# A gather asked for ahead of the accumulating scatter, and a one-hot sum as one matmul, in a mixture-of-experts trunk kernel

## The reference, cut to what matters

```
logits = (tok @ w_router + b_router)
top_logit, top_e = lax.top_k(logits, 4)
gate_w = softmax(top_logit)
# per expert, for the tokens that chose it:
gu = xs @ w_gu[e] + b_gu[e];  g, u = gu[:, :1024], gu[:, 1024:]
g = min(g, 7);  u = clip(u, -7, 7)
act = (u + 1) * (g * sigmoid(1.702 * g))
out = (act @ w_down[e] + b_down[e]) * gate_w
y = segment_sum(out, token)          # four rows are added up for each token
```

## Time and profile before

| | us |
|---|---|
| median of 3 runs | 2640.77 |
| lowest and highest | 2635.83, 2645.7 |
| the profiled execution, its own time | 2641.59 |
| its span, first to last instruction | 2639.9 |
| TensorE busy in the span | 2405.0 (91%) |
| VectorE, ScalarE, GpSimd busy | 1545.6, 1337.7, 835.9 |
| mean granted TensorE clock | 0.965 of full speed |

### The profile page before, as it was taken

One profiled execution on the slowest core, in us unless ns is written; L12 is line 12 of the kernel. 1 busy time (PEld: TensorE's weight loads), 2 busy tenths in 40 slices (PEclk: granted clock), 3 DMA queues, 4 the chain that ended last, 5 costly groups with the idle time before them and its releaser, 6 DMA issues.

```text
span 2639.9 us, 55169 instructions
## 1 busy us (share of the span) xinstructions
PE 2405.0 (91%) x19141; PEld 1347.5 (51%) x19142; DVE 1545.6 (59%) x1828; ACT 1337.7 (51%) x1395; POOL 835.9 (32%) x945
## 2 busy tenths in 40 slices
PE   6999988899989949899899998889988999999991
PEld 3555544667755535455455554445544555545550
DVE  2222246566635665961953768999679715165975
ACT  1111144356532244862843658888678624165861
POOL 1212222410003354343332443434334423233422
PEclk9999989899999969999999999999999999999996
DMA  8000043430032285982964779999989925177974
GB/s 331 11 18 18 9 153 123 125 90 0 0 114 89 96 290 167 388 300 69 361 230 136 263 262 334 397 397 393 332 306 398 331 57 194 28 256 274 356 281 182
DMA packets 180248, 538.48 MB, mean 204 GB/s; under 512 B 20672, under 2 KB 37490, under 8 KB 180142
## 3 DMA queue, kind: packets, MB, share of 16 engines
q1 hardware_dynamic: 150620, 487.79, 48.7%
q0 software_dynamic: 26656, 46.85, 7.9%
q10 hardware_dynamic: 2916, 3.14, 0.4%
HBM read 493.11 MB, written 45.20 MB: 204 GB/s over the span
## 4 chain that ended last, share of the span: by engine, by line
PE 46%; DVE 6%; issue 6%; ACT 2%; DMA 2%; POOL 1%; ACTq 0%; DVEq 0%; POOLq 0%; SPq 0%
PE psum L2054 42%; DVE arena L1825 5%; PE psum L2043 2%; PE psum L2038 2%; PE psum L2032 1%; ACT arena L1647 1%; DMA arena<-in_w_down 1%; DVE arena L1919 0%; DVE arena L1884 0%; DVE arena L1920 0%; DMA expert_lists<-arena 0%; POOL expert_lists L1502 0%; DVE arena L1933 0%; ACT arena L1695 0%; DVE arena L1874 0%
## 5 line engine op out<-in xcount | busy, mean ns | idle before, releaser
L2054 PE MATMUL psum<-arena 128*64 128x512 bf16 x12528 | 1419.0, 382 | 72.2 <-DVE arena L1874 39.4
L2054 PEld LDWEIGHTS psum<-arena 128*64 128x64 bf16 x12528 | 714.3, 111 | 727.1 <-DVE arena L1825 53.7
L1825 DVE TENSOR_TENSOR arena<-arena 128x2048 bf16<-128x2048 f32 x384 | 862.8, 2287 | 184.5 <-ACT arena L1647 184.2
L1647 ACT ACTIVATE arena<-arena 128x2048 bf16<-128x2048 f32 x384 | 723.0, 1904 | 99.0 <-DVE arena L1825 70.0
L1557 POOL DMA_INDIRECT expert_sums<-arena x90 | 186.9, 2076 | 670.7 <-issue 648.2
L551 PE MATMUL psum<-arena 128*128 128x512 f32 (+2 forms) x864 | 298.9, 504 | 1.1 <-ACT arena L407 1.1
L551 PEld LDWEIGHTS psum<-arena 128*128 128x128 f32 x864 | 150.8, 190 | 133.8 <-issue 129.1
L1874 DVE TENSOR_TENSOR arena<-psum,arena 128x512 bf16<-128x512 f32 x87 | 59.9, 688 | 233.6 <-ACT arena L1689 233.6
L1528 POOL DMA_INDIRECT arena<-expert_inputs,arena x88 | 107.5, 1222 | 202.5 <-PE psum L2032 176.9
L1685 ACT ACTIVATE arena<-psum 128x1024 bf16<-128x1024 bf16 x87 | 88.6, 1018 | 154.8 <-issue 152.8
L1700 ACT ACTIVATE arena<-psum,arena 128x512 f32<-128x512 f32 x87 | 59.3, 682 | 202.1 <-PE psum L2054 202.1
(11 more groups left out here) (269 smaller groups left out, 2186.8 us busy)
## 6 DMA issues: line engine op xcount, KB each, us to landing
arena<-in_w_gu SPq DMA_DIRECT2D x256, 1024.0 KB, 16.0
arena<-in_w_down SPq DMA_DIRECT2D x128, 1024.0 KB, 13.8
arena<-in_w_ada SPq DMA_DIRECT2D x12, 2048.0 KB, 9.6
arena<-in_x_sample SPq DMA_DIRECT2D x16, 512.0 KB, 3.4
arena<-in_w_in SPq DMA_DIRECT2D x3, 2048.0 KB, 20.3
expert_sums<-arena SPq DMA_DIRECT2D x10, 512.0 KB, 6.4
expert_inputs<-arena SPq DMA_DIRECT2D x10, 512.0 KB, 2.8
x_after_mixing<-arena SPq DMA_DIRECT2D x9, 512.0 KB, 2.7
```

Of the source, the lines that this page charges most:

```text
L1647: nc.scalar.activation(high(e, p, c), raw[p][c], ACT.Copy).then_inc(sem(f"hi_made{c}"), 1)
L1825: nc.vector.tensor_tensor(w_lo[p][c], raw[p][c], high(e, p, c), ALU.subtract).then_inc(sem(f"lo_made{c}"), 1)
L2054: last = nc.tensor.matmul(bank(b)[group(g)], parts[part][:, cols], w[:, kk, g * H:(g + 1) * H], start=False, stop=(k == KT - 1 and part == 1))
```

## The change

In the body of a unit, `add_up(j)` is moved from behind `shift(j)` to the end, behind `gather(j + 1)`. No wait is added or removed: `add_up` still waits for `taken` and `y_made`, and `gather` for `present_kept` and `x_turned`. For the last unit, which has nothing following, the order is as before.

The one-hot matrix of the first list becomes 128 columns wide (the same 64 places twice), so that one matmul serves both halves, and the row of padding is made by a few more small VectorE instructions.

```diff
-        iota, chosen, tokf = ar(51200, UNIT), ar(51264, UNIT), ar(51328, NT)
-        padrow, first_row, gate0 = r3(ar(51340, 4), 2), ar(51344, 2), ar(51348, TOPK)
+        iota, chosen = ar(51200, 2 * UNIT), ar(51328, 2 * UNIT)
+        padrow, first_row, gate0 = ar(51456, 2), ar(51458, 2), ar(51460, TOPK)
+        tokf, upper_half, pad_twice = ar(51464, NT), ar(51480, 1), ar(51481, 1)
...
                     if following is not None:
                         fetch(*following)
                     shift(j, True)
-                    add_up(j)
                     if following is not None:
                         wait(pool, sem("listed_in"), j * 32 + 32)
                         wait(pool, sem("gathered"), j * 16 + 16)
...
                         nc.gpsimd.tensor_copy(present, listed).then_inc(sem("present_kept"), 1)
                         wait(pool, sem("present_kept"), j + 1)
                         gather(j + 1)
+                    add_up(j)
...
+                nc.vector.tensor_copy(iota[:, UNIT:UNIT + NE], expert)
+                nc.vector.tensor_scalar(iota[:, UNIT + NE:2 * UNIT], expert, float(NE), None, ALU.add)
+                nc.vector.tensor_scalar(upper_half, padid, float(2 * TOK + UNIT), -float(2 * UNIT - 1), ALU.is_ge, ALU.mult)
...
-                nc.vector.memset(padrow[:, :, 1], 0.0)
-                nc.vector.tensor_scalar(padrow[:, :, 0], tokid[:, 0:2], float(2 * TOK), None, ALU.add).then_inc(sem("first_ready"), 1)
+                nc.vector.tensor_scalar(pad_twice, padid, 2.0, float(-2 * TOK), ALU.mult, ALU.add)
+                nc.vector.memset(padrow[:, 1:2], 0.0).then_inc(sem("first_ready"), 1)
                 dve.wait_ge(sem("first_ready"), 1)
+                nc.vector.tensor_tensor(padrow[:, 0:1], pad_twice, upper_half, ALU.add).then_inc(sem("first_ready"), 1)
...
                     wait(pe, sem("first_chosen"), b + 1)
-                    for h in range(2):
-                        last = nc.tensor.matmul(PS[64 * h:64 * h + 64, 3 * H:3 * H + 2], chosen, first_row, start=False,
-                                                stop=(isinstance(b, int) and b == LATE))
-                    last.then_inc(sem("first_summed"), 1)
+                    nc.tensor.matmul(bank(3, 2), chosen, first_row, start=False,
+                                     stop=(isinstance(b, int) and b == LATE)).then_inc(sem("first_summed"), 1)
```

More of the change, by code:

```diff
@@ L1983, in first_sum @@
                     if isinstance(b, int) and b == 0:
-                        wait(pe, sem("first_ready"), 1)
-                        for h in range(2):
-                            nc.tensor.matmul(PS[64 * h:64 * h + 64, 3 * H:3 * H + 2], ident[:, 0:UNIT], padrow[:, h, :], start=True, stop=False)
+                        wait(pe, sem("first_ready"), 2)
+                        nc.tensor.matmul(bank(3, 2), ident, padrow, start=True, stop=False)
                     wait(pe, sem("first_chosen"), b + 1)
-                    for h in range(2):
-                        last = nc.tensor.matmul(PS[64 * h:64 * h + 64, 3 * H:3 * H + 2], chosen, first_row, start=False,
-                                                stop=(isinstance(b, int) and b == LATE))
-                    last.then_inc(sem("first_summed"), 1)
+                    nc.tensor.matmul(bank(3, 2), chosen, first_row, start=False,
+                                     stop=(isinstance(b, int) and b == LATE)).then_inc(sem("first_summed"), 1)
                 turn_mix(0)
```

## The result

The changed kernel is slower: 2674.78 us (median of 5 runs, 2672.67 to 2678.42) against 2642.28 us beside it, a ratio of 1.0123 with a 95% interval of 1.0106 to 1.0140. Its profiled execution took 2678.42 us with a span of 2676.8, which is 36.9 us over the span before. It is the slowest of the five, so that the traces differ by somewhat more than the medians, 32.5 us.

The account below looks back on a forecast made before the run. It took TensorE, busy 91% of the span, as the bound, with division binding five slow stretches. Terms 9 + 12 + 8 + 4 + 0 = 33 us on 2641.59 gave 2674.6, stated as 2674; range 2646 to 2698.

Parts of the forecast that it names:

- The chain: Behind the scatter: it lands late, the shift's copies and `taken` follow late, then `result` and ScalarE's work behind it.
- What the move can gain: nothing, since the gather waits for TensorE: Body of a unit: for 74 of 88 gathers no gain, as each starts after TensorE turns the previous input.
- Scatter at +2.2: GpSimd, each unit: scatter starts 2.2 us after the input's turning ends, 6.8 us later than at -4.6.
- Landing 8.8 us later: Scatter's landing, 8.8 us after its start (median), at +11.0 us from the end of the unit's turning.
- Entries and insides of the slow stretches, 12 + 8 us: Five stretches where divisions bound TensorE: late results cost 2.4 us per entry, 1.5 us inside each; 12 and 8 us.
- First units of experts of two, 1.5 us each, 9 us: First unit of six two-unit experts: result 2.9 us late, TensorE stands 1.5 us each, 9 us in all.
- the bound of 15 us for the term: High bound for the six two-unit experts' first units, 15 us, if the landing misses another division.
- The start, 4 us: Start of the expert stage: first gather gains 3.5 us, second turning loses it; 4 us lost, bounds -3.5 and 8.
- TensorE's waits for low activations and divided weights grow by 25 us together: TensorE, as a sign in the trace: waits for low activations (39.4 us before) and divided weights grow some 25 us together.
- GpSimd's loop closes: GpSimd's chain from gather to `present` copy takes 12 to 17.3 us within a 17.34 us period; rival that it bounds: 0.07.
- The first list, 0 us: Routing's first list: one matmul replaces two and small VectorE instructions are added; 0 us, bounds -1 and +2.
- The rule of the Trainium skill: Scatter's landing by the skill page: 2.6 us for 256 KB, leaving only the start's gain, about 2638 us.

Follow-up runs that it names:

- e1: The kernel before with only the scatter moved behind the gather, the first list's old two-matmul sum kept: 2677.15 us, ratio 1.0131.
- e8: The changed kernel with `result` taking its gate from `moved`, waiting for the shift's first copy instead of all three: 2660.51 us, ratio 1.0062.
- e2: The kernel before with only the first list's 128-column one-hot sum, the scatter left where it was: 2643.33 us, ratio 1.0005.
- e5: The changed kernel with `result` written behind up to two more `hi` (ScalarE's half of a division) of its unit: 2679.09 us, ratio 1.0138.
- e9: The changed kernel with `result` waiting for the shift's first copy alone and written behind up to two more `hi`: 2639.00 us, ratio 0.9991.
- e7: The kernel before, in its old order, with `result` written behind up to two more `hi` of its unit: 2644.63 us, ratio 1.0007.

## Why the prediction was right, point by point

- **The forecast**, 2674 with a range of 2646 to 2698: measured 2674.78. The chain was right; the nearness is luck, as the terms show: the start was 5 us too high, the first units 9 us too low, and the clock stood in no term.
- **What the move can gain: nothing, since the gather waits for TensorE**. Right: it starts 0.9 us behind the turning in both kernels.
- **Scatter at +2.2.** Right where nothing divides (+2.24 in the unit shown). In units into which late divisions reach, the gather's own instruction takes longer (median of all 1568 ns against 1007 ns before), and the scatter starts at +2.7 to +4.4, in four units later still. This was not foreseen.
- **Landing 8.8 us later**. Right in the middle only. In the 44 units with a late result the landing takes 8.9 us in the median, but under 8 in 15 of them; over all units the median is 5.9. In the very unit that the prediction priced it took 6.9: landed at +9.1 and not +11.0. The third copy, said to be free, was held there as well, so that the result came 2.6 us late against 2.9 said. Two errors met, and the stall of 1.32 us against 1.5 is luck as well.
- **Entries and insides of the slow stretches, 12 + 8 us.** Measured 18.8, and each stretch is 2.3 to 5.1 us longer, against about 4 said. But some 9 of the 18.8 are slower matmuls, which the prediction did not price. Single results were later than said (4.4 us at the entry shown in place of 2.4, because the scatter started at +3.0), and some of it was absorbed.
- **First units of experts of two, 1.5 us each, 9 us.** This term was mis-sized: what lies outside the slow stretches measured 17.7 us. Of the six units three cost the unit behind them 1.3 to 1.5 us, as said (one of them, unit 6, lies in the sum of its stretch) and one not at all. But two stalls are of 7.0 and 5.7 us (4.06 and 3.87 of standing, and 2.7 and 1.7 of a product at the lower clock), and one of 2.0 stands behind a slow stretch, where I had none. Ahead of all three of these a result came at +16.7 to +17.0, with all three copies held. I had this case as the bound of 15 us for the term, "if it misses another", and it went beyond it, since the clock came on top.
- **The start, 4 us.** Wrong step, and of the wrong sign: from the first turning on, units 0 and 1 are 1.35 us shorter. The 0.1 us of the account above holds a first turning that came later for another reason. The gain was 1.2 us at the second turning in place of 3.5, and the loss behind it did not come: the waits are 7.80 and 0.34 us, against 6 and 6 to 10 said. The same 1.2 us stand in e1 and e8, whose unit 0 is 23.3 and 23.4 us long, against 24.5 before and in e2; e5 and e9, in which `result` is written later, have 24.5 too, and why is open. I had the copy to `present` wait only for a division, until 975.3; it waited for the fetched list, which landed at 977.5. Before, the scatter's instruction hid that landing. The second gather landed just in time (0.34 us).
- **TensorE's waits for low activations and divided weights grow by 25 us together.** Right: 39.4 to 62.8 and 31.3 to 30.0, which is 22 us. But the experts lost 35.1.
- **The clock, no term.** The sum prices standing alone. Slower matmuls made 14.3 us of the 35.1. The standing, which is what the sum priced, is 20.8 us, against 33 forecast.
- **GpSimd's loop closes.** Right: TensorE's wait for gathers stays at the start (5.90, 7.80 and 0.34 us).
- **The first list, 0 us.** Right, by e2.
- **The rule of the Trainium skill** ("DMA: Bandwidth & Descriptors", "Anatomy of one DMA — SWDGE (gpsimd) path"), by which an estimate for this scatter is 2.6 us, would have made the change free. The trace disagrees: the scatter's landing took 4.5 to 9.9 us in the changed kernel.

What remains open: why some scatters land in 5 us and some in 9 to 10. They go with the weight loads' traffic: in the changed kernel the loads' queue moves 0 to 179 GB/s in the first 5 us of the 46 scatters that land in under 6 us, and 262 to 358 GB/s in those of the other 44. But no run here took the loads away. The standing in the two large stalls I explain by three held copies; e8, which removes two copies, has 1.3 and 1.0 us in those units in place of 7.0 and 5.7, but a stall of 4.1 us in another (unit 85: 2.26 us of standing, and the same 7.06 us for 48 matmuls), so that single stalls depend on how a landing falls among the divisions.

## What to carry to other kernels

When an instruction is moved on an in-order engine, ask first which wait it is moved behind: here a gather that takes 1 us carried a wait, and together they made the scatter 6.8 us late. Follow the landing of the moved transfer to the one who waits for it last, and price it by what is written behind that waiter on its own engine, for a late result was free (e7) and a standing ScalarE was not. Count what a stall of TensorE costs behind it too: here the clock fell, and two stalls of 4 us cost 7.0 and 5.7. And take from such a chain what the waiter doesn't need: letting it wait for the first of three small copies, and writing work that is ready ahead of it, made the same late scatter harmless (e9).

## What the runs showed of the hardware

A copy of six columns on GpSimd takes 0.19 us, or up to 2.3 us while VectorE runs divisions with two inputs in SBUF: it is held until the division under way ends, and three copies in a row are held by three divisions (1832.70 to 1837.76 above). I had reckoned with this. What I had not expected is that it works back: feeding VectorE better (e5) held GpSimd longer and cost as much as it gave. Writing the requests of a gather is held as well, up to 3.2 us in place of 1.0: all of the 48 gathers that take over 1.2 us in the changed kernel end 0.9 us behind the end of a division.

The granted clock of TensorE was 0.51 for 6.8 us, from 1807.3 on, while TensorE had stood from 1804.6 to 1808.65; 48 matmuls of the same shape took 8.11 us there and 5.37 us at the full clock.
